# Hybrid decoder layer on one Trainium2 core: identity made on chip, x in another order, ones sums and gate rows on column groups, bias transposes moved

## What is computed

```python
proj = x @ w_in                                   # q, k, v, z, beta/gate columns, and dq, dk, dv
qkv  = silu(causal_depthwise_conv(gq, gk, gv))    # 4 taps
q, k = l2_normalize(q), l2_normalize(k)           # x * rsqrt(sum(x*x) + 1e-6), per token and head
beta = sigmoid(gb); g = -exp(a_log) * softplus(ga + dt_bias)
o    = gated_delta_rule_chunked(q, k, v, g, beta) # decay = exp(cumsum(g)[i] - cumsum(g)[j])
od   = differential_attention(dq, dk, dv, lam)
x = layer_norm(ALPHA * x + concat(rms_norm(o) * silu(z), rms_norm(od)) @ w_out)
x = layer_norm(ALPHA * x + mem_cross_attention(x, mem))
x = layer_norm(ALPHA * x + moe_ffn(x))            # top 4 of 32 experts, softmax over the chosen
# moe_ffn of an expert: clamped_swiglu(xb @ w_gate + b_gate, xb @ w_up + b_up) @ w_down + b_down
```

## Time and profile before

| | us |
|---|---|
| median of 3 runs | 1222.14 (1220.93 to 1222.97) |
| the profiled execution | 1222.16 |
| its span in the trace | 1220.3 |
| TensorE busy | 1074.5 (88%) |
| VectorE busy | 314.7 (26%) |
| ScalarE busy | 188.5 (15%) |
| GpSimd busy | 23.4 (2%) |
| DMA, 446.45 MB | mean 366 GB/s |

### The profile page before, as it was taken

How to read it: one execution, slowest core, us unless ns; L and a number is a source line. 1 busy time by engine, 2 the same in 40 slices (tenths; PEclk the granted TensorE clock), 3 DMA queues, 4 the chain that set the end, 5 groups by cost and what they waited for, 6 DMA issues and landing times.

```text
span 1220.3 us, 19780 instructions
## 1 busy us (share of the span) xinstructions
PE 1074.5 (88%) x7593; PEld 487.8 (40%) x7594; DVE 314.7 (26%) x980; ACT 188.5 (15%) x431; POOL 23.4 (2%) x32
## 2 busy tenths in 40 slices
PE   7999999999889999879796979796979797888886
PEld 6776874964423333323232323232323232322322
DVE  1857433222512222212121212121212121212123
ACT  0231431120111111111010101110101110101111
POOL 0110010100000000000000000000000000000000
PEclk9999999999999999999899989898979898989898
DMA  9743140588899999999999999999999999999996
GB/s 356 262 173 138 70 167 15 207 317 346 326 428 429 426 428 430 429 428 428 429 428 429 430 428 428 427 429 428 429 430 429 428 429 428 429 428 430 430 428 260
DMA packets 44904, 446.45 MB, mean 366 GB/s; under 512 B 6976, under 2 KB 7568, under 8 KB 20176
## 3 DMA queue, kind: packets, MB, share of 16 engines
q1 hardware_dynamic: 40784, 442.30, 86.4%
...
HBM read 445.06 MB, written 1.05 MB: 366 GB/s over the span
## 4 chain that ended last, share of the span: by engine, by line
PE 53%; DMA 39%; DVE 4%; issue 2%; DVEq 1%; ACT 1%; SPq 1%; ACTq 0%; PEldq 0%
DMA main<-in_exp_w_up_dram 38%; PE bank L1422 18%; PE bank L931 7%; PE bank L1480 6%; PE bank L921 6%; PE bank L1270 2%; PE bank L1189 2%; PE bank L1348 2%; PE bank L1462 1%; PE bank L980 1%; DVEq L1985 1%; PE bank L961 1%; DVE kst L1991 1%; DVE main L1988 1%; DVE main L1978 1%
## 5 line engine op out<-in xcount | busy, mean ns | idle before, releaser
L1422 PE MATMUL bank<-main 128*32 128x512 f32 x3008 | 383.1, 663 | 106.4 <-DMA main<-in_exp_w_up_dram 101.4
L1422 PEld LDWEIGHTS bank<-main 128*32 128x32 f32 x3008 | 113.6, 120 | 369.2 <-issue 368.2
L1480 PE MATMUL bank<-main,kst 128*32 128x512 f32 x1504 | 180.6, 598 | 16.8 <-DVE kst L1991 16.8
L1978 DVE TENSOR_TENSOR main<-bank,main 128x256 f32<-128x256 f32 x94 | 39.6, 421 | 572.4 <-PE bank L1462 572.4
L1393 PE MATMUL bank<-main 64*128 64x512 f32 x384 | 95.4, 615 | 0.7 <-ACT main L869 0.7
L849 ACT ACTIVATE main<-bank 128x512 f32<-128x512 f32 x46 | 27.5, 598 | 437.5 <-PE bank L1422 437.1
L931 PE MATMUL bank<-main 128*128 128x512 f32 x192 | 84.0, 593 | 0.3 <-ACT main L723 0.3
L1480 PEld LDWEIGHTS bank<-main,kst 128*32 128x32 f32 x1504 | 39.3, 109 | 90.4 <-issue 64.3
L921 PE MATMUL bank<-main 128*128 128x256 f32 x320 | 70.6, 380 | 0.0
L921 PEld LDWEIGHTS bank<-main 128*128 128x128 f32 x320 | 60.4, 190 | 8.8 <-issue 0.8
L1348 PE MATMUL bank<-main,kst 128*32 128x256 f32 x752 | 52.3, 389 | 2.9 <-DVE kst L1889 2.0
...
## 6 DMA issues: line engine op xcount, KB each, us to landing
main<-in_exp_w_gate_dram SPq DMA_DIRECT2D x64, 2048.0 KB, 32.3
main<-in_exp_w_up_dram SPq DMA_DIRECT2D x64, 2048.0 KB, 36.8
main<-in_exp_w_down_dram SPq DMA_DIRECT2D x63, 2048.0 KB, 38.5
main<-in_w_in_dram SPq DMA_DIRECT2D x6, 2048.0 KB, 21.6
main<-in_xa_wk_dram SPq DMA_DIRECT2D x2, 2048.0 KB, 11.1
main<-in_w_out_dram SPq DMA_DIRECT2D x2, 2048.0 KB, 11.1
main<-in_xa_wv_dram SPq DMA_DIRECT2D x2, 2048.0 KB, 10.5
main<-in_xa_wq_dram SPq DMA_DIRECT2D x2, 2048.0 KB, 13.1
```

The costliest lines, as they stand in the source:

```text
L1422: last = pe.matmul(gu_bank[at:at + CAP, :], xg_chunk(k), weights(role, k, f), start=(k == 0), stop=(k == KC - 1))
L1480: last = pe.matmul(y_bank[at:at + CAP, :], hT[:, j, f, :], weights(role, j, h), start=(f == 0 and pair == 0), stop=(f == 1 and pair == 1))
L1978: return tt(dst, gT[:, :, w, :, :], b.unsqueeze(3).broadcast_to([P, 4, 2, CAP]), ALU.add)
```

## The change

1. The identity is no longer loaded. GpSimd sets 128 x 128 ones and keeps the diagonal with an affine select.
2. TensorE makes seven products of the identity with itself before the first transposes and three after the second set, into bank 7, whose contents nobody reads.
3. SP issues x's first half, two w_in pieces, x's second half, two w_in pieces. ScalarE issues its first half of x first, its second behind the small columns.
4. R is one bank: eight products with 32 weight columns (`gB` is only 32 columns wide), head h on partitions 32h to 32h+31. VectorE copies it, and four products, each of 32 rows whose first alone is one (`first_row`), write it to all partitions of four banks R0 to R3. They stand between the two halves of z1.
5. The sums of squares are one bank ss, made by four products with 32 weight columns. ScalarE takes one logarithm and one exponential. Four products of 32 rows spread the result to the banks norm0 to norm3, between the two halves of dqk0. VectorE scales q and k from those banks.
6. The bias DMAs are issued when wo3 is filled, into a part of `conv_in`, and the bias transposes follow pos, where begin_sum(1) was. begin_sum(1) goes to begin_sum(2) and (3).
7. The first selection reads pos from its bank; the copy of pos and the subtraction of the block size come after the normalisation.
8. GpSimd waits for the two pieces of the last w_down load and raises the semaphore of that load's slot, ahead of its last two roots.

```diff
@@ unit_table
-    u += [("z0", "A"), ("gcum", "D"), ("R0", "D"), ("R1", "D"), ("z1", "A")]
-    u += [(f"ss{i}", "A") for i in range(4)]
+    u += [("z0", "A"), ("gcum", "D"), ("R", "D")] + [(f"R{h}", "D") for h in range(4)] + [("z1", "A"), ("ss", "A")]
+    u += [(f"norm{i}", "D") for i in range(4)]
...
-LAST_USE = {"xgT0": "pos", "cum": "rt1", "etab": "x2T3", "GT": "etab", "acc2": "wo3", "acc3": "rt0"}
+LAST_USE = {"xgT0": "pos", "cum": "rt1", "etab": "x2T3", "GT": "etab", "bT": "x2T2", "acc1": "bT", "acc2": "wo3", "acc3": "rt0"}
@@ sync
+            load_x(0)
+            load_first_rows(0)
+            load_first_rows(1)
+            load_x(1)
+            load_first_rows(2)
+            load_first_rows(3)
@@ gpsimd
+            pool.memset(ident, 1.0)
+            pool.drain()
+            pool.affine_select(out=ident, in_=ident, pattern=[[-1, P]], compare_op=ALU.is_equal, fill=0.0, base=0,
+                               channel_multiplier=1).then_inc(ident_ready, 1)
...
+            for i in range(2):
+                pool.wait_ge(last_down[i], 16)
+            pool.sem_inc(odd_full[D1], 16)
@@ scalar
-            act.dma_start(ident, d["consts"][:, K_ID:K_ID + P]).then_inc(ld_ident, 16)
...
-            for i in range(4):
-                empty(f"ss{i}", sq_mem[:, 512 * i:512 * (i + 1)], func=ACT.Ln, bias=eps_rms)
...
+            empty("ss", sq_mem[:, 0:512], func=ACT.Ln, bias=eps_rms)
+            act.wait_ge(act_emptied, emptied("ss")[1])
+            act.activation(sq_mem[:, 0:512], sq_mem[:, 0:512], ACT.Exp, scale=-0.5).then_inc(l2_exp, 1)
...
+            act.wait_ge(unit_filled, UNIT_AT["wo3"] + 1)
+            for w, n in enumerate(["exp_b_gate", "exp_b_up"]):
+                act.dma_start(bias_rows[:, HALF * w:HALF * (w + 1)], d[n][0].rearrange("e (f c) -> (e f) c", f=2)).then_inc(ld_bias, 16)
@@ tensor
-            pe.wait_ge(ld_ident, 16)
+            pe.wait_ge(ident_ready, 1)
+            stay_busy(banks[7], 7)
...
             x_T(0)
             x_T(2)
+            stay_busy(banks[7], 3)
...
+            ps = begin("R")
             for g in range(TB):
-                ps = begin(f"R{g}")
                 for h in range(HEADS):
-                    last = pe.matmul(ps[:, h * P:(h + 1) * P], gB[:, 4 * g + h, :], upper, start=True, stop=True)
-                last.then_inc(unit_filled, 1)
-            token_major("z1", xT, 1, through(2, 3), 512)
+                    last = pe.matmul(ps[32 * h:32 * h + 32, g * P:(g + 1) * P], gB[:, 4 * g + h, :], upper, start=True, stop=True)
+            last.then_inc(unit_filled, 1)
+            token_steps("z1", xT, 1, through(2, 3), 512, range(0, 4))
+            need("R")
+            pe.wait_ge(row_ready, 1)
+            for h in range(HEADS):
+                ps = begin(f"R{h}")
+                row = slice(32 * h, 32 * h + 32)
+                pe.matmul(ps[:, 0:256], first_row[row, :], gcum_rows[row, :], start=True, stop=True).then_inc(unit_filled, 1)
+            token_steps("z1", xT, 1, through(2, 3), 512, range(4, 8)).then_inc(unit_filled, 1)
...
-                pe.matmul(ps[:, :], ones, sq_mem[:, 512 * i:512 * (i + 1)], start=True, stop=True).then_inc(unit_filled, 1)
+                last = pe.matmul(ps[32 * i:32 * i + 32, :], ones[:, 0:32], sq_mem[:, 512 * i:512 * (i + 1)], start=True, stop=True)
...
-            dqk_unit(0)
+            bank_dqk0 = begin("dqk0")
+            dqk_part(bank_dqk0, 0, 0)
+            pe.wait_ge(l2_exp, 1)
+            for i in range(4):
+                ps = begin(f"norm{i}")
+                row = slice(32 * i, 32 * i + 32)
+                pe.matmul(ps[:, :], first_row[row, :], sq_mem[row, 0:512], start=True, stop=True).then_inc(unit_filled, 1)
+            dqk_part(bank_dqk0, 0, 1).then_inc(unit_filled, 1)
...
-            pe.wait_ge(qk_normed, 4)
+            need("norm3")
@@ vector
-                stt(part, part, GDN_DK ** -0.5 if i < 2 else 1.0, sq_mem[:, 512 * i:512 * (i + 1)],
-                    ALU.mult, ALU.mult).then_inc(qk_normed, 1)
+                stt(part, part, GDN_DK ** -0.5 if i < 2 else 1.0, filled(f"norm{i}")[:, :],
+                    ALU.mult, ALU.mult).then_inc(dve_emptied, 1)
...
-            select(0)
+            for b in range(TB):
+                last = ts(selw[:, b, :], iota[:, 0:CAP], ps[:, 32 * b:32 * b + 1], M2[:, b, 0:1], ALU.is_equal, ALU.mult)
+            last.then_inc(sel_ready, 1)
+            dve.drain()
             finish_half(0)
             finish_half(1)
 
+            dve.tensor_copy(pos, counts_ps[:, 0:64])
```

102 lines of the change are left out of this document (60 added, 42 removed).

## The result

The changed kernel takes 1230.31 us in the median of 18 runs (1226.52 to 1252.15), the kernel before 1222.51 (18 runs, 1220.93 to 1224.61). The ratio is 1.0067, 95% interval 1.0052 to 1.0082: slower by 7.8 us, where 4.5 us less were forecast. Ratios here leave out runs more than 1.5% above a kernel's fastest, so where the runs of a kernel fall into two groups the text gives the groups beside the median. The profiled execution took 1232.91 us, 10.75 more than that of before.

A forecast was written before the change was run, and what follows sets the result against it. TensorE's chain was taken to bind until the chosen expert weights start streaming at 320.53 us, then DMA. Terms 1.0 + 0.8 + 1.3 + 1.1 + 0.3 = 4.5; 1222.16 - 4.5 = 1217.7 us, range 1216.4 to 1221.4.

The forecast's parts named there:

- The frame: After the first chosen w_gate load at 320.53 us, fixed bytes at fixed rate; earlier TensorE gains count one for one.
- Rival D: Something unseen, such as code fetch, takes the gain before the expert stream starts at 320.53; about 1222 us, chance 8%.
- The start, 1.0: First product on the 2 MB load moves from 18.83 to about 17.8 us, bound by that load; 1.0 us won.
- Rival A: The clock falls in the start's new 2.4 to 2.8 us pause, losing 1.7 us; 1219.4 us, chance 30%.
- R, 0.8: R on column groups, then spread from 32 rows: 0.53 us each in place of 1.89; 0.8 us won.
- the sums, 1.3: Attention's sums of squares grouped, then spread, in place of 3.43 us, with 0.15 us exponential wait; 1.3 us won.
- the 0.96 of the sum: Time taken for four spreading products of 512 columns on row groups in the sums of squares: 0.86 + 0.1 us.
- Bias transposes, 1.1: Bias transposes leave TensorE's chain at 258.91 us; ScalarE, out of its issue at 265.29, leaves the whole 1.1 us won.
- The choice of block 0, 0.3: Selection reads pos from its bank, 0.4 us sooner to the first gate load's release; 0.3 us won after bias wait.
- rival C: Biases land late, at 320.9 us, and the moved transposes at 311.4 wait; slower, 1227.2 us, chance 4%.
- I take 0.1: Cost allowed for the late bias landing at the moved transposes, with landing bounds of 308.4 and 313.6 us.
- the upper bound of 313.6: Half way case: biases land only as the big w_down load ends, costing 2.2 us; 1219.9 us, chance 8%.

The follow-up runs named there:

- e13: The changed kernel with sixteen one-column products added in TensorE's pause ahead of the 2 MB load at 17.75 us; median 1234.46 us.
- e1: The changed kernel with the bias DMAs, bias transposes and begin_sum(1) back where they stood before; median 1224.66 us, ratio 1.0014.
- e6: The changed kernel with the bias loads issued early, when the mixer is done, and four late transposes of 128 rows; median 1226.21 us.
- e18: The changed kernel with router_w alone loaded where the mixer is done; median 1228.35 us.
- e3: The kernel before with only the on-chip identity, the ten identity products and the new load order of x; median 1228.43 us, ratio 1.0048.
- e2: The kernel before with only the bias DMAs, bias transposes and begin_sum(1) moved as in the change; median 1227.62 us, ratio 1.0046.
- e12: The changed kernel with biases as before, no early GpSimd slot release, early rank table, fifteen one-column and one 512-column products in the start's pause; 1220.23 us.
- e14: e13 with the bias loads issued early, as in e6; median 1233.41 us.
- e15: e14 with the rank table loaded early as well, as in e9; median 1228.30 us.
- e9: The kernel before with ScalarE's rank table load moved from behind router_w's load to where the mixer is done; median 1223.42 us, ratio 1.0006.
- e16: e15 with router_w loaded where the mixer is done; median 1220.87 us, ratio 0.9995.
- e7: e3 with three products of 512 columns added in TensorE's pause ahead of the 2 MB load; median 1225.03 us, ratio 1.0024.
- e17: e12 with router_w loaded where the mixer is done; median 1220.76 us, ratio 0.9990.
- e5: The kernel before with 36 idle semaphore increments added in TensorE's wait for x; median 1227.90 us, ratio 1.0043.

## Why the prediction was wrong, step by step

Three steps failed, and one cost had no term (the splitting, below). The three are that the time behind F is fixed, that the biases land early enough behind pos, and that the 1.1 us of their transposes stays won.

**The frame.** "What follows it is a fixed number of bytes at a fixed rate" is the step that hid most. It holds for the stream (some 901 us behind F), but only if TensorE releases the slots of the first two blocks in time. The changed kernel released them 5.1 us late, because its TensorE program is 70 instructions longer and the code for the loop's entry was not there (e13). The prediction had the standstill of 3.17 us in front of it, used it as a row on the clock, and did not ask what it was. Rival D named code fetch, but only as something that takes the gain, at 8% and 1222. It can take more than the gain.

**The start, 1.0.** Right in place and size (17.75; 17.8 forecast). Rival A, with 30%, came true in the profiled run, and its price was right: 1.7 forecast, 1.77 measured. It came true in e1, e6 and e18 too, and not in e3.

**R, 0.8, and the sums, 1.3.** The four row groups do run together. Spreading 512 columns took 1.07 to the next start, R 0.57, spreading R 0.65, the sums 0.99, and TensorE did not wait for the exponential. The two gains are 0.65 and 1.38 by themselves. The Trainium skill, "TensorE: Matmul & The Clock Gate", table at the end, gives 3.07x for such a set of four; 3.43 us over the measured 1.12 us in the chain is 3.06, so the trace agrees with the page and not with the 0.96 of the sum. What the sum left out is the splitting: z1 in two halves is 3.63 + 3.63 in place of 6.86, dqk0 3.70 + 3.56 in place of 6.91. That is 0.75 together, and the two terms gave 1.28 in place of 2.1. The sum had no term for it.

**Bias transposes, 1.1.** The step failed: TensorE was 2.25 us ahead at 258.62 (260.87 before), and 0.35 ahead at the router. The prediction took 265.29, where ScalarE comes out of its issue, as a time that leaves 1.1 us of room, computed from a TensorE that had won nothing yet. With 1.0 us won ahead of it and 1.1 here, TensorE arrived first and waited 1.67, and the block itself ended later (266.04). Terms that are each hidden from their neighbour one by one are not hidden together. And taking the transposes away sent a weight load out 1.1 us sooner against router_w: the one loss that nothing in the prediction pointed to, though the 15.0 us of router_w's load said how it fares among weights.

**The choice of block 0, 0.3, and rival C.** "I take 0.1" was wrong. The load landed at 314.38, behind the upper bound of 313.6, a case that had only 8%. (The bound is itself 0.6 above its rows: 305.46 + 7.5 is 313.0.) The price was wrong as well: the wait itself is 1.73, but the profiled run lost 6.4 between the last projection and F, since the clock was low for 17 us. How much of that the wait brought about is open: in the changed kernel the clock fell before it, in e2 within it. Without the wait (e6) F was 6.9 sooner in the profiled run and the median 4.1 lower. The term itself held: from the last pos product to the second half of the gather it is 2.75 us before and 2.34 in e6, 0.4 less.

**The clock in the router's products (T2)** is settled only so far: in five of the 20 profiled executions (changed, e3, e12, e14, e15) it fell within 0.7 us of the end of the router's last sixteen records of 32 columns, with TensorE busy. In e9 and e16 it fell a little later, behind waits of under 1 us, and in e2, e13 and e18 in the wait for the biases or just behind it. In ten it stayed up, among them e1, e6, e7 and e17 with like timing. One traced execution of each kernel does not tell whether an edit brings it about. F is 1.4 us later in e12 than in e17, and 2.0 in e3 than in e7.

**The balance by the runs.** Edit 6 costs 5.6 us (e1); about 2 of them go when router_w's load is moved (e18, which frees ScalarE as well), about 4 with the biases (e6), and the two overlap. The code at the loop's entry costs 3 to 5 (S of the changed kernel, e1, e3 and e18 against 41.3; e5 and e13 for the cause). In medians, e12 is 4.4 us below e1, with the rank table early as well. Against them stands the little that was won and not swallowed (0.35 us at the last projection of the profiled run). The parts add up to 8 to 10, a little over the 7.8, and their overlap was not measured. Edit 8 has no run of its own; behind F + S the changed kernel is 0.36 us shorter, so little can be its. With all four obstacles out of the way the whole change is worth 1.35 us (e16, against 1222.22 in the same series) of the forecast 4.5; the best five runs of e15 show 2.7 to 4.3 us. Between those and e16 lie the 1.3 us that TensorE waits for ScalarE in e16 and, in its profiled execution, a low clock from 311.6 to 317.9; the runs do not divide the difference between them.
